# Pairing the first layer's gates and the later attention heads' projections as seven half-width products

## The chip, the cores and the metric

The kernel runs on one core of a Trainium2 chip. The metric is device time in microseconds. Before the change the median of three runs is 1910.99 us.

## The reference, cut to what matters

Two transformer blocks run one after the other on x of 512 tokens and 1024 features, all in fp32. The first block is:

```
h = rmsnorm(x, norm_mix_g);  proj = h @ w_in      # mLSTM q,k,v,o; attention q,k,v; gates g_a,g_b
y_a = mlstm(...)                                  # 4 heads
y_b = dilated window attention                    # 3 groups x 8 heads; head pairs hp = 0..3
merged = sigmoid(g_a) * (y_a @ w_proj_a) + sigmoid(g_b) * (y_b @ w_proj_b)
x = x + merged @ w_out
x = x + (silu(hf @ w_gate) * (hf @ w_up)) @ w_down    # hf = rmsnorm(x, norm_ffn_g)
```

The second block mixes gated linear attention and sparse attention and has its own feed-forward. The change doesn't touch it.

## The kernel before, in words

**Units.** Every weight matrix is cut into units of 1024 x 128 (eight pieces of 128 x 128, 512 KB). `unit_order` writes out the order by hand: 0 is the first. A unit with activations transposed (features on partitions, 512 tokens as columns) gives 128 output features. fp32 accuracy comes from a split into two fp32r parts: for each of the eight k a unit issues WH x XH, WH x XL and WL x XH (`products`, lines 1561 to 1563). That is 24 matmuls of 512 columns.

**Preparing a weight.** SP loads the unit into one of three RAW buffers (`load`, five units ahead). ACT copies it to WH (`split`, line 2064), and DVE (line 2467) or POOL (line 3267) writes WL = RAW - WH, two units ahead. WH and WL have three buffers each, which the code counts as six halves of 512 columns (`place_weights`). `lo_on_pool` gives POOL the odd units of some kinds.

**Pairs.** In the two feed-forwards most gate and up units already run in pairs. A pair is two neighbouring units seen as a 2 x 2 block matrix, tokens split in halves of 256. Seven products replace eight (Winograd's form of Strassen's scheme): `pair_products`, lines 1637 to 1639, 7 products of 12 matmuls of 256 columns. The seven weight operands ("chunks", half a unit each) are `a11, a12, s1, a22, s2, s4, s3`. Four of them are sums or differences made in place in the raw buffers (`chunk_add`, DVE). ACT copies each chunk to its WH half (line 2073), and DVE writes its WL half (line 2499). The activations' seven forms lie in AR. The products are put together by `pair_keep` (ACT), `pair_held` and `pair_add` (DVE) from four PSUM banks.

**The stages that matter here.** (1) mLSTM, four heads, with the projections of the next head as fill. (2) ga/pa: eight gate units `ga` and eight projection units `pa` in turn, `ga0 pa0 ga1 ...`, with four PSUM banks. (3) Attention: four head pairs hp of four query blocks. While hp is worked on, the nine q, k, v units of hp + 1 are the fill (`Fill`, a quarter of a unit at a time); for hp = 3 the eight `gb` units are. At the end of a block stand, in this order, the scores of the next block on PE, its softmax on DVE, its exponentials on ACT, and the PV product and the transposes of P. The fill has banks 0 and 1 only. Banks 2 and 3 hold scores, 4 the unfolded strips, 5 the PV product, and 6 and 7 transposes. (4) `pb`: eight units of 512 x 128, merged with `gb`, then the eight `out` units, which add to XT. XT stays in SBUF from the start until then.

Every engine runs its own list in order and waits on semaphores, so an instruction that waits holds everything behind it on its engine. The evictions of `qa, ka, va, gb, ga` read PSUM once and multiply by RB (the root, DVE lines 2613 and 2614).

Of the kernel before, what the change touches and what calls it, by code (L numbers as in the profile page):

```python
# [8 lines left out]
S = 512  # L9
# [13 lines left out]
LO_ON_POOL = ()  # L23
WARM_START = 9
# [34 lines left out]
def unit_order():  # L59
# [100 lines left out]

def lo_on_pool(i):

    return i % 2 == 1 and i > 3 and i != 7 and UNITS[i][0] in BUSY_DVE or i == AT["gate2", 1, 0]
# [11 lines left out]
def pair_start(i):  # L175

    name, j = UNITS[i][:2]
    if name[-1] == "2":
        return i - j % 2 if name in ("gate2", "up2") and "2" in PAIRED and j >= PAIR_FROM else None
# [3 lines left out]
def place_weights():  # L183
# [3 lines left out]
    for i in range(len(UNITS)):  # L187
# [10 lines left out]
        elif p == i:  # L198
            chunks = [((i, c), (h + c,), ("prod", i, c)) for c in range(7)]
        else:  # L200
            continue
# [10 lines left out]
def place_raw():  # L212
# [3 lines left out]
    for i, (name, j, k0, nk) in enumerate(UNITS):  # L216
        if name in ("if", "small2"):
            continue
        x = order.pop(0)
# [49 lines left out]
class Order:  # L269
# [35 lines left out]
    small_products = small_evict = small_select = keep_warm = gates_products = gates_evict = gates_select = none  # L305
    pair_products = pair_keep = pair_held = pair_add = pair_silu = pair_hi = pair_lo = none
# [109 lines left out]
def ahead(e, i):  # L416
    if i + 2 < len(UNITS):
        e.split(i + 2)
# [201 lines left out]
def mlstm(e):  # L620
# [25 lines left out]
    for h in range(4):  # L646
# [6 lines left out]
        fill.quarters(12 if h else 8)  # L653
        for t in range(4):
            e.hold((*SB, OB)[t], "numer", h, t)
        e.numerators(h)
        fill.quarters(6)
        e.normed(h)
        e.turns_apart = h < 3
        fill.quarters((6, 10, 10, 10)[h])  # L660
        if h == 3:
            mlstm_scores(e, 4)
# [31 lines left out]
def attention_blocks(e):  # L694
# [3 lines left out]
    at, e.turns_apart = unit_of("qa", 1), True  # L698
    for m, (hp, b) in enumerate(items):
        if b == 0:  # L700
            n = 9 if hp < 3 else 8
            fill = Fill(e, range(at, at + n), 4 if hp < 3 else 7)
            at += n
# [18 lines left out]
        if hp and b == 0:  # L722
            e.hold(4, "unfolded", hp - 1)
# [12 lines left out]
    e.hold(4, "unfolded", 3)  # L736
# [6 lines left out]
    fill.drain(True)  # L743
# [11 lines left out]
def attention(e):  # L755
# [4 lines left out]
    for j in range(8):  # L760
        unit(e, unit_of("ga", j))
        unit(e, unit_of("pa", j))
# [4 lines left out]
    attention_blocks(e)  # L767
# [24 lines left out]
def pair_steps(at, end):  # L792
# [3 lines left out]
    for i in range(at, end):  # L796
        nk, p = UNITS[i][3], pair_start(i)
        if p == i:
            steps += [("pair", i, c) for c in range(7)]
# [327 lines left out]
def build(nc, xT_d, wst_d, con_d, col_d, relb_d, oh_d, wa2_d, w1_d, w2_d, out_d, scr_d, mx_d):  # L1127
# [6 lines left out]
    with ExitStack() as ctx:  # L1134
        def sb(name, shape, dt=f32):
            return ctx.enter_context(nc.sbuf_tensor(name, shape, dt))

        XT = sb("XT", [128, 8, 512])
# [16 lines left out]
        RC = sb("RC", [128, 16])  # L1155

# [21 lines left out]
        pool_done = {n: signal("pool_" + n) for n in ("norm", "mlstm", "ffn", "gla")}  # L1178
        raw_in = [signal(f"raw_in{i}", 16) for i in range(NR)]
# [5 lines left out]
        wa2_in, w1_in, w2_in = signal("wa2_in", 16), signal("w1_in", 16), signal("w2_in", 16)  # L1185
        out_done = [signal(f"out_done{i}", 16) for i in range(2)]
# [33 lines left out]
        def plain(which, j, n=512):  # L1220

            at_ = H_at + 2048 * (8 * "HH HL AH AL".split().index(which) + j)
            return nc.alloc_sbuf_tensor_at(f"{which}plain{j}", [128, n], f32, offset=at_)[:, :]
# [44 lines left out]
        sgt = SS[0][:, 0:512]  # L1268
# [64 lines left out]
        def raw(i):  # L1333

            return RAW[:, R_SLOT[i], :]
# [8 lines left out]
        twice_held = bass.AP(HELD.tensor, HELD.offset, [list(HELD.ap[0]), [0, 2], [1, 256]])  # L1344

# [43 lines left out]
        def gate_tile(i):  # L1389
# [4 lines left out]
            return {"ga": sgt, "gb": gb3[:, j, :], "mg": SGT, "mn": SN3[:, j, :]}[name]  # L1394
# [45 lines left out]
        class Sync(Order):  # L1440
# [17 lines left out]
            def load(s, i):  # L1458
# [8 lines left out]
                d.then_inc(*raw_in[R_SLOT[i]].next("raw", i))  # L1467

# [63 lines left out]
        class Tensor(Order):  # L1532
# [87 lines left out]
            def pair_products(s, sfx, i, c):  # L1620
# [3 lines left out]
                          4: (("sum_z", i), 256), 5: (("sum", i), 256), 6: (("sum_w", i), 0)}[c]  # L1624
                out = PS[:, s.bank[key], o:o + 256]
                if c in (0, 1, 2, 6):
                    s.free(*key)
                elif c == 4:
                    pe.wait_ge(*at("kept", i))
                pe.wait_ge(*at("lo", i, c))  # L1630
                wh, wl = chunk(WH, i, c), chunk(WL, i, c)
                for m in range(4):
# [101 lines left out]
            def after(s, i, p):  # L1734
# [1807 lines left out]
```

## Time and profile before

| | |
|---|---|
| runs | 1910.97, 1910.99, 1911.03 us |
| span of the profiled execution | 1909.1 us |
| granted TensorE clock | 1.000 (2.4 GHz) |
| PE busy | 1898.5 us, 99% |
| DVE, ACT, POOL busy | 66%, 39%, 14% |

The span is that of one profiled execution. Its whole time isn't listed apart; the median of the runs is 1.9 us above the span, which is what lies around it. A busy share of a pipelined PE says only that matmuls follow one another; the distance between two starts gives their price.

### The profile page before, as it was taken

What the parts mean: (1) busy time and instruction counts of PE and PEld (TensorE: products, weight loads), DVE (VectorE), ACT (ScalarE), POOL (GpSimd) and SP (SyncE); (2) the same over time, 40 slices, a digit from 0 to 9 for tenths busy, and PEclk for the clock granted to TensorE, in tenths of its full rate; (3) what the DMA queues carried; (4) which work ended last, traced back from release to release, by engine and by line L of the source; (5) the groups of instructions that cost most, each with busy time, mean ns of one, the idle gap of its engine ahead of it and who ended that gap; (6) DMA issues with size and microseconds to landing.
All of it is one profiled execution on the core that took longest, in us unless ns stands there. A gap on an engine that the chain in (4) does not pass through costs nothing.

```text
span 1909.1 us, 26308 instructions
## 1 busy us (share of the span) xinstructions
PE 1898.5 (99%) x10599; PEld 1591.0 (83%) x10599; DVE 1255.4 (66%) x1894; ACT 735.3 (39%) x1265; POOL 265.1 (14%) x156
## 2 busy tenths in 40 slices
PE   9999999999999999999999999999999999999998
PEld 7788888888888888999997778877777878899998
DVE  7777543345455748777776756766776667887874
ACT  6332322233334444344435522224444354444442
POOL 0211210111111113000004001121111133100002
PEclk9999999999999999999999999999999999999999
DMA  5322233232321323233333222322121322333332
GB/s 177 102 70 85 88 86 115 89 99 67 89 67 45 115 91 104 78 106 102 114 108 103 77 67 78 100 79 65 56 67 40 116 79 87 100 100 100 100 130 81
DMA packets 53472, 172.77 MB, mean 90 GB/s; under 512 B 5963, under 2 KB 10643, under 8 KB 53352
## 3 DMA queue, kind: packets, MB, share of 16 engines
q1 hardware_dynamic: 52912, 170.66, 28.8%
q8 instruction: 84, 1.38, 0.3%
q10 hardware_dynamic: 440, 0.44, 0.1%
q14 instruction: 36, 0.29, 0.1%
HBM read 168.86 MB, written 2.22 MB: 90 GB/s over the span
## 4 chain that ended last, share of the span: by engine, by line
PE 94%; DVE 3%; ACT 1%; POOL 1%; issue 0%; DVEq 0%
PE PS L1561 22%; PE PS L1563 22%; PE PS L1562 22%; PE PS L1637 5%; PE PS L1639 5%; PE PS L1638 5%; PE PS L1983 1%; PE PS L2005 1%; PE PS L1780 1%; PE PS L1795 1%; PE PS L1961 1%; PE PS L1841 1%; PE PS L1827 1%; PE PS L1818 1%; PE PS L1748 1%; POOL XT L3338 1%
## 5 line engine op out<-in xcount | busy, mean ns | idle before, releaser
L1561 PE MATMUL PS<-HH,WH 128*128 128x512 f32 x1124 | 444.0, 395 | 0.8 <-DVE WL L2467 0.7
L1563 PE MATMUL PS<-HH,WL 128*128 128x512 f32 x1124 | 438.0, 390 | 0.0
L1562 PE MATMUL PS<-HL,WH 128*128 128x512 f32 x1124 | 437.4, 389 | 0.0
L2064 ACT ACTIVATE WH<-RAW 128x1024 fp32r<-128x1024 f32 (+2 forms) x256 | 261.1, 1020 | 336.4 <-PE PS L1563 271.4
L2467 DVE TENSOR_TENSOR WL<-RAW,WH 128x1024 fp32r<-128x1024 f32 (+2 forms) x195 | 251.2, 1289 | 113.7 <-ACT WH L2064 112.0
L1561 PE MATMUL PS<-AH,WH 128*128 128x512 f32 x816 | 323.7, 397 | 0.0
L1563 PE MATMUL PS<-AH,WL 128*128 128x512 f32 x816 | 318.1, 390 | 0.0
L1562 PE MATMUL PS<-AL,WH 128*128 128x512 f32 x816 | 317.6, 389 | 0.0
L1561 PEld LDWEIGHTS PS<-HH,WH 128*128 128x128 f32 x1124 | 211.1, 188 | 49.7 <-issue 4.2
L1563 PEld LDWEIGHTS PS<-HH,WL 128*128 128x128 f32 x1124 | 211.0, 188 | 45.1
L1562 PEld LDWEIGHTS PS<-HL,WH 128*128 128x128 f32 x1124 | 211.2, 188 | 42.2 <-issue 0.2
L3267 POOL TENSOR_TENSOR WL<-RAW,WH 128x1024 fp32r<-128x1024 f32 (+1 forms) x61 | 139.0, 2279 | 740.1 <-ACT WH L2064 740.1
L1637 PE MATMUL PS<-AR,WH 128*128 128x256 f32 x784 | 219.6, 280 | 0.0
L1639 PE MATMUL PS<-AR,WL 128*128 128x256 f32 x784 | 218.8, 279 | 0.0
L1638 PE MATMUL PS<-AR,WH 128*128 128x256 f32 x784 | 218.8, 279 | 0.0
L1561 PEld LDWEIGHTS PS<-AH,WH 128*128 128x128 f32 x816 | 153.2, 188 | 37.1 <-issue 6.5
L1563 PEld LDWEIGHTS PS<-AH,WL 128*128 128x128 f32 x816 | 153.2, 188 | 33.0
L1562 PEld LDWEIGHTS PS<-AL,WH 128*128 128x128 f32 x816 | 153.4, 188 | 30.5 <-issue 0.5
L2613 DVE TENSOR_TENSOR AR<-PS,RB 128x512 f32<-128x512 f32 (+2 forms) x117 | 84.3, 723 | 134.5 <-PE PS L1563 128.0
L2073 ACT ACTIVATE WH<-RAW 128x512 fp32r<-128x512 f32 x196 | 119.4, 624 | 93.3 <-DVE RAW L2486 36.7
L1637 PEld LDWEIGHTS PS<-AR,WH 128*128 128x128 f32 x784 | 147.2, 188 | 1.1
L1638 PEld LDWEIGHTS PS<-AR,WH 128*128 128x128 f32 x784 | 146.7, 187 | 1.1
(360 smaller groups left out, 2260.7 us busy)
## 6 DMA issues: line engine op xcount, KB each, us to landing
RAW<-wst SPq DMA_DIRECT2D x292, 512.0 KB, 3.6
RAW<-wst SPq DMA_DIRECT2D x16, 256.0 KB, 2.6
RAW<-wst SPq DMA_DIRECT2D x8, 384.0 KB, 3.1
XT<-xT SPq DMA_DIRECT2D x3, 512.0 KB, 7.3
out<-XT SPq DMA_DIRECT2D x4, 384.0 KB, 2.5
AR<-mx SPq DMA_DIRECT2D x4, 256.0 KB, 6.2
AR<-scr SPq DMA_DIRECT2D x16, 64.0 KB, 4.3
AR<-scr SPq DMA_DIRECT2D x8, 128.0 KB, 4.8
```

The costliest lines, as they stand in the source:

```text
L1561: T.matmul(out, wh, XH[:, k, :], start=k == 0, stop=False)
L1562: T.matmul(out, wh, XL[:, k, :], start=False, stop=False)
L1563: m = T.matmul(out, wl, XH[:, k, :], start=False, stop=k == nk - 1)
L1637: T.matmul(out, wh[:, w], xh, start=m == 0, stop=False)
L1638: T.matmul(out, wh[:, w], xl, start=False, stop=False)
L1639: t = T.matmul(out, wl[:, w], xh, start=False, stop=m == 3)
L1748: t = T.transpose(PS[:, b, q * 128:(q + 1) * 128], src[:, q * 128:(q + 1) * 128], ident())
L2064: t = A.activation(whole(WH, i, n), raw(i)[:, 0:n], ACT.Copy, scale=1.0)
L2073: t = A.activation(chunk(WH, i, c), raw_chunk(i, c), ACT.Copy, scale=1.0)
L2467: t = V.tensor_tensor(whole(WL, i, n), raw(i)[:, 0:n], f(whole(WH, i, n)), ALU.subtract)
L2613: return V.tensor_tensor(dst, src, rb, ALU.mult)
L3267: t = G.tensor_tensor(whole(WL, i, n), raw(i)[:, 0:n], f(whole(WH, i, n)), ALU.subtract)
```

## The change

Twenty pairs are added to those of the feed-forwards (`MIXED`): four in `ga`, four in `gb`, and four in the nine projection units of each of hp 1, 2 and 3 (the ninth stays whole). `ga` and `pa` now come two and two. The pairs' products run in the order a11, a12, s1, a22, s2, s3, s4 (`PAIR_ORDER`), so that three banks do: the product of s3 goes into the half of `sum_z` that `pair_keep` has read. In attention `sum_z` is bank 4, and the unfolded strips move to bank 5.

The half sums of the activations (T1, T4, T5, T6 of each of four m) are made in mLSTM's last head: `t_sums` (DVE, two scalings of 512 columns and four sums of 256), `t_hi` (ACT, 1024), `t_lo` (POOL, 1024). Their high part TXH lies on XT, so `reload_x` loads XT again (2 MB, four DMAs of 512 KB on SP's queue) once the product s3 of the last `gb` pair is done, ahead of the loads of pb5 and later.

In the new pairs POOL writes all seven WL halves and does two of the four chunk sums; DVE does the other two. A pair's outputs go to SBUF first (`pair_middle`, `pair_sum`), and `pair_out` multiplies them by RB from there. There are two more raw buffers from hp 1's projections to the `gb` units, on the free halves of AL. The list of fill is one `Stream` of steps for ga/pa and attention, of which `Share` hands out 32 steps for a head and 28 for the last.

```diff
-    for j in range(8):
+    for j in range(0, 8, 2):
         add("ga", j)
+        add("ga", j + 1)
         add("pa", j)
+        add("pa", j + 1)
...
+PAIR_ORDER = (0, 1, 2, 3, 4, 6, 5)
+ADD_ON_POOL = (5, 6)
+def mixed_pairs():
+    starts = [AT["ga", j, 0] for j in range(0, 8, 2)] + [AT["gb", j, 0] for j in range(0, 8, 2)]
+    starts += [AT["qa", hp, 0] + x for hp in (1, 2, 3) for x in (0, 2, 4, 6)]
+    return {p + n: p for p in starts for n in (0, 1)}
...
+class Stream:
+    def prepare(self):
+        e = self.e
+        while self.chunks and all(self.done.get(y, -1) < self.n for y in W_BEFORE[self.chunks[0]]):
+            while self.n_add < min(2, len(self.chunks)):
+                e.chunk_add(*self.chunks[self.n_add])
+                self.n_add += 1
+            self.n_add -= 1
+            y = self.chunks.pop(0)
+            e.chunk_hi(*y)
+            e.chunk_lo(*y)
+            if y[0] >= self.end:
+                break
+    def step(self):
+        e, (kind, i, x) = self.e, self.steps[self.n]
+        if kind == "pair":
+            if x == 0:
+                e.load(i + 5)
+                e.load(i + 6)
+            if x == 0 and len(e.ring) == 2:
+                e.hold(4, "sum_z", i)
+            elif x in (0, 1, 2):
+                e.sum_bank("sum" if x else "sum_z", i + (x == 2))
+            e.pair_products("1", i, x)
...
+        now, self.queue = self.queue, []
+        for i2, y in now:
+            e.pair_out(i2, y)
...
+        self.prepare()
...
+            if x == 0:
+                e.pair_keep(i)
+            elif x == 6:
+                e.pair_middle(i)
+            if x in (6, 5):
+                e.pair_sum(i, int(x == 6))
+                self.queue.append((i, int(x == 6)))
...
+            def pair_middle(s, i):
+                V.tensor_tensor(held[:, 0:256], z[:, 256:512], kept[:, 0:256], ALU.add).then_inc(
+                    *dve_done["attn"].next("held", i))
+                dve.wait_ge(*at("held", i))
+                t = V.tensor_tensor(held[:, 256:512], z[:, 0:256], held[:, 0:256], ALU.add)
+                t.then_inc(*bank_read.next("free", "sum_z", i))
...
+            def chunk_lo(s, i, c):            # POOL
+                pool.wait_ge(*at("hi", i, c))
+                t = G.tensor_tensor(chunk(WL, i, c), raw_chunk(i, c), f(chunk(WH, i, c)), ALU.subtract)
+            def chunk_add(s, i, c):           # POOL
+                pool.wait_ge(*at("added", i, 4))
+                if c == 5:
+                    pool.wait_ge(*at("lo", i, 1))
+                    t = G.tensor_tensor(r1[:, 512:1024], r1[:, 512:1024], r1[:, 0:512], ALU.add)
+                else:
+                    pool.wait_ge(*at("lo", i, 3))
+                    t = G.tensor_tensor(r2[:, 512:1024], r1[:, 0:512], r2[:, 512:1024], ALU.add)
...
+            def reload_x(s):
+                sp.wait_ge(*at("prod", unit_of("gb", 6), 6))
+                for g in range(4):
+                    d = S.dma_start(XT[:, 2 * g:2 * g + 2, :], xT_d[:, 2 * g:2 * g + 2, :])
...
-        e.hold(4, "unfolded", 3)
+        e.hold(OB, "unfolded", 3)
```

The DVE's own `chunk_add` for s2 is as before: it waits for the WL half of a11, which POOL now writes.

## Rows read from the trace of the kernel before

**Rows 1.** The page: engines' busy time, then the chain that ended last.
```profile
PE 1898.5 (99%) x10599; PEld 1591.0 (83%) x10599; DVE 1255.4 (66%) x1894; ACT 735.3 (39%) x1265; POOL 265.1 (14%) x156
...
PE 94%; DVE 3%; ACT 1%; POOL 1%; issue 0%; DVEq 0%
```

**Rows 2.** Windows (columns: PE, PEld, DVE, ACT, POOL busy, clock, DMA): stages around the change.
```profile
200.00:300.00 100.00, 100.00 (x458) 82.34 (x457) 48.08 (x68) 24.99 (x35) 15.54 (x8) 1.00 0.34 99
...
286.00:370.00 84.00, 84.00 (x372) 69.57 (x372) 30.99 (x38) 20.08 (x23) 2.40 (x1) 1.00 0.35 104
...
429.00:494.00 65.00, 64.95 (x402) 53.39 (x400) 31.29 (x45) 20.95 (x51) 11.92 (x5) 1.00 0.29 77
...
625.00:652.00 27.00, 26.93 (x119) 21.97 (x118) 22.94 (x31) 11.20 (x17) 4.32 (x3) 1.00 0.40 127
```

**Rows 3.** Timeline of PE: first matmul of unit pa0, and of the next unit.
```profile
288.67 0.39 PE L1561 MATMUL PS<-AH,WH 128*128 128x512 f32 x1
...
294.11 0.39 PE L1561 MATMUL PS<-HH,WH 128*128 128x512 f32 x1
```

**Rows 4.** Timeline of PE: first and 84th matmul of a feed-forward pair, and the next.
```profile
853.38 0.28 PE L1637 MATMUL PS<-AR,WH 128*128 128x256 f32 x1
...
863.15 0.28 PE L1639 MATMUL PS<-AR,WL 128*128 128x256 f32 x1
863.27 0.40 PE L1561 MATMUL PS<-HH,WH 128*128 128x512 f32 x1
```

**Rows 5.** Chain in order of time: scores, transposes and PV at block ends.
```profile
414.01 1.08 PE PS L1818 x12
415.08 1.02 PE PS L1841 x16
416.11 1.02 PE PS L1827 x8
429.38 0.87 PE PS L1818 x12
...
494.09 0.87 PE PS L1818 x12
```

**Rows 6.** POOL by line and shape, whole span.
```profile
L3267 POOL TENSOR_TENSOR WL<-RAW,WH 128x1024 fp32r<-128x1024 f32 x53 | 127.8, 2412 | 685.7 <-ACT WH L2064 685.7
...
L3267 POOL TENSOR_TENSOR WL<-RAW,WH 128x512 fp32r<-128x512 f32 x8 | 11.2, 1402 | 54.4 <-ACT WH L2064 54.4
```

**Rows 7.** Timeline of POOL in the pb stage, then six additions after another.
```profile
634.80 1.29 POOL L3267 TENSOR_TENSOR WL<-RAW,WH 128x512 fp32r<-128x512 f32 x1 [3.71 <-ACT WH L2064]
...
1553.18 9.82 POOL L3338 TENSOR_TENSOR XT<-XT,AR 128x512 f32<-128x512 f32 x6 [3.50 <-DVE AR L3172]
```

**Rows 8.** Timeline of DVE beside the POOL work of rows 7.
```profile
634.99 1.65 DVE L2651 TENSOR_TENSOR AR<-AR 128x512 f32<-128x512 f32 x1
...
1558.36 0.74 DVE L3172 SCALAR_TENSOR_TENSOR AR<-AR,COL,PS 128x512 f32<-128x512 f32 x1
1559.02 1.13 DVE L2446 SCALAR_TENSOR_TENSOR HL<-XT,COL,HH 128x512 fp32r<-128x512 f32 x1
```

**Rows 9.** DVE by line and shape, 750 to 1000 us (feed-forward pairs).
```profile
L2486 DVE TENSOR_TENSOR RAW<-RAW 128x512 f32<-128x512 f32 x14 | 9.6, 685 | 0.0
...
L2555 DVE TENSOR_TENSOR AR<-PS,AR 128x256 f32<-128x256 f32 x14 | 5.8, 417 | 0.0
```

**Rows 10.** The page's groups: ACT's copy of a chunk.
```profile
L2073 ACT ACTIVATE WH<-RAW 128x512 fp32r<-128x512 f32 x196 | 119.4, 624 | 93.3 <-DVE RAW L2486 36.7
```

**Rows 11.** Timeline of ACT after the scores of rows 5.
```profile
417.70 0.51 ACT L2249 ACTIVATE AR<-AR 128x256 f32<-128x256 f32 x1 [7.06 <-DVE AR L2904]
...
420.44 1.05 ACT L2064 ACTIVATE WH<-RAW 128x1024 fp32r<-128x1024 f32 x1
```

**Rows 12.** DMA queue (packets, MB, share of 16 engines), and issue to landing.
```profile
q1 hardware_dynamic: 52912, 170.66, 28.8%
...
RAW<-wst SPq DMA_DIRECT2D x292, 512.0 KB, 3.6
```

More of the change, by code:

```diff
@@ L177, in pair_start @@
     name, j = UNITS[i][:2]
+    if i in MIXED:
+        return MIXED[i]
     if name[-1] == "2":
@@ L198, in place_weights @@
         elif p == i:
-            chunks = [((i, c), (h + c,), ("prod", i, c)) for c in range(7)]
+            order = PAIR_ORDER if i in MIXED else range(7)
+            chunks = [((i, c), (h + n,), ("prod", i, c)) for n, c in enumerate(order)]
         else:
@@ L218, in place_raw @@
             continue
+        if i == AT["qa", 1, 0]:
+            order += [NR, NR + 1]
+            user[NR] = user[NR + 1] = [("unit", AT["pa", 7, 0])]
+        elif i == AT["pb", 0, 0]:
+            order = [x for x in order if x < NR]
         x = order.pop(0)
@@ L305 @@
     small_products = small_evict = small_select = keep_warm = gates_products = gates_evict = gates_select = none
+    t_sums = t_hi = t_lo = pair_middle = pair_sum = pair_out = reload_x = none
     pair_products = pair_keep = pair_held = pair_add = pair_silu = pair_hi = pair_lo = none
@@ L759, in attention @@
     e.load_bias(1)
-    for j in range(8):
-        unit(e, unit_of("ga", j))
-        unit(e, unit_of("pa", j))
+    stream = Stream(e, unit_of("ga", 0), unit_of("gb", 7) + 1, 4)
+    for _ in range(60):
+        stream.step()
     e.ring = [0, 1]
@@ L789, in ffn, with __init__, finish @@
         unit(e, i)
-def pair_steps(at, end):
+class Stream:
+    def __init__(self, e, at, end, ready):
+        self.e, self.end, self.n = e, end, 0
+        self.steps, self.done = pair_steps(at, end, True), {}
+        for n, (kind, i, x) in enumerate(self.steps):
+            self.done[("prod", i, x) if kind == "pair" else ("unit", i)] = n
+        self.chunks = [(i, c) for i in range(at, end + 2) for c in ([None] if pair_start(i) is None else
+                                                                    PAIR_ORDER if pair_start(i) == i else [])][ready:]
+        self.n_add, self.queue = 0, []
+    def prepare(self):
[21 more added lines that the diff above has]
+            e.pair_products("1", i, x)
+        else:
+            if x[0] == 0:
+                e.load(i + 5)
+                e.sum_bank("sum", i)
+            e.products(i, x)
+        now, self.queue = self.queue, []
+        for i2, y in now:
+            e.pair_out(i2, y)
+            if UNITS[i2 + y][0] in PARTS:
+                e.later.append(("unit", i2 + y, 1))
+        self.prepare()
+        if kind == "unit":
+            if x[-1] % 4 == 3:
+                flush(e, not e.turns_apart)
+            if x[-1] == 7:
+                evict(e, i)
+        else:
+            if x in (1, 3, 4, 5):
+                flush(e, not e.turns_apart)
+            if x == 0:
[5 more added lines that the diff above has]
+                self.queue.append((i, int(x == 6)))
+            if x == 5 and len(e.ring) == 2:
+                e.taken += 1
+        self.n += 1
+    def finish(self):
+        e = self.e
+        for i2, y in self.queue:
+            e.pair_out(i2, y)
+            if UNITS[i2 + y][0] in PARTS:
+                e.later.append(("unit", i2 + y, 1))
+        self.queue = []
+        self.prepare()
+        while self.chunks:
+            self.n += 1
+            self.prepare()
@@ L795, in pair_steps @@
+def pair_steps(at, end, quarters=False):
     steps = []
@@ L798, in pair_steps @@
         if p == i:
-            steps += [("pair", i, c) for c in range(7)]
+            steps += [("pair", i, c) for c in (PAIR_ORDER if quarters else range(7))]
+        elif p is None and quarters:
+            steps += [("unit", i, range(2 * q, 2 * q + 2)) for q in range(4)]
         elif p is None and nk == 6:
@@ L1344, in build, with temps, evicted @@
         twice_held = bass.AP(HELD.tensor, HELD.offset, [list(HELD.ap[0]), [0, 2], [1, 256]])
+        T_IN, T_SUM = [plain("AH", 6, use="scaled"), plain("AH", 7, use="scaled")], plain("AL", 6, 1024, "sums")
+        GA_TEMPS = parts(4608, 512, 512, 512, 512)
+        AT_TEMPS = [plain("AH", j, use="held") for j in (4, 5, 6, 7)]
+        SPARE = [plain("AL", j, 1024, use="raw") for j in (4, 6)]
+        def temps(i):
+            if i not in MIXED:
+                return KEPT, HELD, GATE if UNITS[i][0][0] == "g" else [UP, UP]
+            t = GA_TEMPS if UNITS[i][0] == "ga" else AT_TEMPS
+            return t[0], t[1], t[2:4]
+        def evicted(i):
+            return ("out", i) if i in MIXED else ("free", "sum", i)
         def f_tiles(i):
@@ L1847, in unfold @@
                 pe.wait_ge(*at("strips", hp))
-                t = T.matmul(PS[:, 4, 0:64], con("unfold"), strips, start=True, stop=True)
+                t = T.matmul(PS[:, OB, 0:64], con("unfold"), strips, start=True, stop=True)
                 t.then_inc(*pe_done["attn"].next("unfolded", hp))
```

218 lines of the change are left out of this document (186 added, 32 removed).

## The prediction

> **What bounds the kernel now.** I read the page first. PE is busy 99% of 1909.1 us and holds 94% of the chain that ended last; no other engine has over 3% of it [rows 1]. A busy share alone isn't enough, so I took windows over the stages that the change touches: PE has no idle time in ga/pa or in attention, and 0.07 us of 27 in pb [rows 2]. The clock is 1.00 throughout. So a matmul taken away shortens the kernel by its pitch, as long as nothing makes PE wait. POOL is almost idle there (2.4 us of 84 in ga/pa, 11.9 of 65 in a head), and DVE is under half busy [rows 2]. The question is whether the two can carry what the change gives them.
>
> **What the change takes from PE.** A whole unit is 24 matmuls; the next unit starts 294.11 - 288.67 = 5.44 us later [rows 3], so two units cost 10.88 us. A pair of seven products is 84 matmuls of half width, and the work behind it starts 863.27 - 853.38 = 9.89 us later [rows 4]: 0.118 us a matmul, 1.41 us a product. The pair saves 0.99 us. Twenty pairs save 19.8 us: 4.0 in ga, 11.9 in the three heads, 4.0 in gb. That is the most that can come back.
>
> **What it adds, pair by pair.**
> - *POOL.* Seven WL halves and two chunk sums, nine operations of 512 columns. Alone one takes 1.29 us [rows 7]; the mean of the eight such operations is 1.40 [rows 6]. The low value is free of DVE's share, which I add apart: 9 x 1.29 = 11.6 us.
> - *DVE with two SBUF inputs.* Two chunk sums and two `pair_out`, four operations of 0.69 [rows 9]. They don't run beside POOL. In rows 8 an addition of normally 0.69 took 1.65 us: it started 0.19 after POOL's operation of 1.29 and ended 0.55 after it. Where POOL ran six operations on end with one such DVE operation to each, it took 9.82 us, 1.64 each [rows 7], and DVE's took 1.13 [rows 8]: one DVE operation costs POOL 1.64 - 1.29 = 0.35 us. I take 0.4, as strided outputs of groups 1 and 2 are longer: 4 x 0.4 = 1.6 us a pair. The bounds are 0 (DVE falls into POOL's gaps) and its whole 0.69.
> - *DVE from PSUM.* Three operations of 256 columns at 0.42 and two of 512 at 0.69 [rows 9], 2.6 us, beside POOL. They replace two evictions.
> - *ACT.* Seven copies of 0.62 [rows 10] for two of 1.05 [rows 11], and one `pair_keep`: some 2.7 us more per pair. ACT is a third busy (20.9 of 65) [rows 2], so only its order matters, below.
>
> The Trainium skill (SBUF - State Buffer, who interferes with whom) says that a DVE instruction with two SBUF inputs and a GpSimd instruction that reads SBUF exclude each other for the whole instruction. The trace agrees that they exclude each other; that DVE costs POOL its whole 0.69 is not what the six operations show.
>
> **ga/pa.** A period is now one pair and two whole `pa`, 9.89 + 10.88 = 20.8 us. POOL and the port need 11.6 + 1.6 us, and DVE's WL of two `pa` and two one-source scalings some 2 us more. Followed chunk by chunk from the end of the first `pa` (s1 and a22 get their halves there, s2 and s3 when the second ends and the pair starts, at 0): the WL of s2 is done at 0.62 + 1.29 and some waiting, 2.1 us, and PE asks at 5.7; POOL's sum for s4 and the WL of s3 end at 4.9, and PE asks at 7.1; the WL of s4 ends at 6.3, and PE asks at 8.5. DVE's operations take about 1 us of these 2.2 to 3.6 us. Four banks leave time. Stall 0, gain 4.0.
>
> **Attention, a head.** PE now needs 28 x 1.41 = 39.6 us for four pairs, 5.4 for the whole unit, and what attention itself costs: 64.7 (494.09 - 429.38, scores to scores [rows 5]) less nine units (49.0), 15.7 us. That is 60.7 us.
>
> (a) *Throughput.* The 28 products with three of four block ends are 39.6 + 11.8 = 51.4 us. POOL and DVE on the port need 4 x (11.6 + 1.6) = 52.8. They fall 1.4 us behind, and catch up during the whole unit.
>
> (b) *Order.* At a block's end ACT waits for DVE's softmax and then makes the exponentials: scores end at 415.09 [rows 5], ACT is back at weights at 420.44 [rows 11], 5.35 us later, while PE is back at products after the transposes and PV, 2.04 us later [rows 5]. Six halves let five products be ready ahead. ACT is back 3.3 us into them, the next chunk's copy and WL take 0.62 + 1.29, so it is ready at 5.2, or 5.8 with a DVE operation in between; PE asks at 5 x 1.41 = 7.07. No stall by that alone. But `sum_z` has one bank. The next pair's first product waits for `pair_middle`, whose two operations (0.84) can start only after the product of s3; and DVE's list has the next pair's sum for s2 ahead of them, which waits for POOL's WL of a11 of that pair. After that WL come on average 0.65 for POOL's next operation, 0.69 and 0.84: 2.2 us, where the margin is 1.3 to 1.9. I take 0.9 us of stall per head. Bounds: 0, and with no lead at all 1.29 + 0.69 + 0.84 = 2.8 us at every pair, of which a POOL that gains from each stall lets about half stand, 1.5.
>
> So a head stalls 1.4 + 0.9 = 2.3 us. The gb stage has the same four pairs under the last head; I give it 2.3 as well. Four stages: 9.2 us.
>
> **The rest.** `t_sums` is 4 x (2 x 0.42 + 4 x 0.42) = 10 us of DVE, with 4 x 1.05 on ACT and 4 x 2.4 on POOL [rows 6]. Its cover is the last mLSTM head, where DVE is 48% and POOL 16% busy [rows 2]: 0, at most 1 us. Without the cover it would be 10 us. `reload_x` puts 2 MB ahead of pb5's load on SP. At 170.66 MB in 28.8% of 1909.1 us, 310 GB/s [rows 12], 2 MB take 6.8 us. Issued 1.4 before gb ends, they are in by 7.4 after it at the latest (2 us of latency), and pb5's 256 KB by 8.5. ACT asks for it at the start of pb3, 3 x 2.72 = 8.2 us in, and PE at 13.6: 0, at most 3. The wait of `out` for XT comes over 20 us in. The unfolded strips in bank 5 wait for a PV product read before on the same list: 0. The two more raw buffers keep SP's loads early; a load of 512 KB takes 3.6 us [rows 12] and has a pair's time.
>
> **Sum.** 19.8 - 9.2 = 10.6 us. Span 1909.1 - 10.6 = 1898.5; with the 1.9 us around it, the same as the gap to the median of the runs shown, 1900.4 us.
>
> **Rivals.**
> - *All is hidden* (0.22). DVE finds gaps in POOL, and the lead of five products absorbs the bursts. For it: over a whole head the port needs 52.8 + 2 of 60.7 us. Against it: the deficit within the 28 products. 1911.0 - 19.8 = 1891.2 us.
> - *The one bank decides: slower* (0.15). Each of the 16 pairs in attention waits 1.5 us for the chain WL of a11, sum for s2, `pair_middle`. 19.8 - 4 x 1.4 - 24 = -9.8: 1920.8 us. It decides from (19.8 - 5.6) / 16 = 0.9 us a pair. For it: POOL has nearly no slack, so the lead is often short. Against it: after a stall the lead is longer.
> - *The port is held for DVE's whole operation* (0.08). 16 x 4 x (0.69 - 0.4) = 18.6 us more: 1919.0 us. Against it: rows 7 and 8. This is what the Trainium skill's rule (SBUF - State Buffer, who interferes with whom) would make of it.
> - *The reload makes pb wait* (0.10): 3 us more, 1903.4 us. For it: the margin at ACT is under 1 us.
> - The forecast has 0.45, with a range of its own of 1896 to 1906.
>
> **How the numbers follow.** Measurements of this kernel tell 0.2%, 3.8 us, from no change: 1907.2 to 1914.8 us. Faster: the forecast but for 0.03, all hidden and the late reload, 0.74. Same: that 0.03, and 0.05 of the two slower cases, should they come in part. Slower: the other 0.18 of them. The range starts a little under all hidden, 1890.5, and goes up to 1912, half way into the slower ones, which leaves out about 0.18.
>
> **What would show it.** PE: 20 x 84 more matmuls of 256 columns, 20 x 48 fewer of 512, at unchanged pitch. ga/pa shorter by 4.0 us. Scores to scores near 63.0 in place of 64.7; under 61 says all is hidden, over 65 one of the slower cases. POOL near 12.9 to 13.5 us a pair, with single operations of 1.6 to 2.0 us where DVE cuts in, and DVE operations with two SBUF inputs of up to 1.9. PE's first wait at a pair's first product, released by DVE, says (b); PE waits inside a pair, released by POOL's WL, say (a). I am wrong if POOL's operation on a RAW and a WH half runs much slower when it never pauses, or if ACT's list, not POOL's, is late.

## The result, and the profile after

The kernel got slower: 1957.86 us (median of four, 1956.66 to 1958.07) against 1911.01 us for the kernel before beside it, ratio 1.0243, 95% interval 1.0231 to 1.0256. The forecast was 1900.4 us, and 1957.86 lies outside the range too. The page of the kernel after, busy times and the chain that ended last:

```profile
PE 1901.3 (97%) x11319; PEld 1626.4 (83%) x11319; DVE 1350.3 (69%) x2034; ACT 781.6 (40%) x1389; POOL 488.9 (25%) x324
...
PE 82%; DVE 7%; POOL 4%; ACT 3%; issue 3%; DMA 0%; SPq 0%; DVEq 0%; ACTq 0%; POOLq 0%
```

Against [rows 1], PE was to be 19.8 us less busy and is 2.8 us more, and its share of the chain fell from 94% to 82%. The span is 1956.0 us. PE's idle time is 1956.0 - 1901.3 = 54.7 us, before 10.6: 44.1 us of new waits. Its busy time should have been 1898.5 - 19.8 = 1878.7 us and is 22.6 us more. So -19.8 + 44.1 + 22.6 = 46.9 us, which is the whole difference of the spans. Windows of the kernel after (PE, PEld, DVE, ACT, POOL busy, clock, DMA): ga/pa, two stretches inside the heads, then 280 to 760 us as a whole:

```profile
286.00:370.00 84.00, 79.55 (x491) 71.91 (x489) 41.01 (x56) 26.53 (x42) 40.54 (x32) 0.98 0.35 108
380.00:445.00 65.00, 55.23 (x425) 50.64 (x425) 40.17 (x51) 25.16 (x61) 51.09 (x36) 0.95 0.26 82
445.00:517.00 72.00, 63.86 (x544) 59.31 (x544) 48.37 (x70) 29.61 (x75) 52.33 (x36) 0.98 0.24 74
280.00:760.00 480.00, 435.58 (x3081) 392.19 (x3081) 293.48 (x405) 189.93 (x408) 267.59 (x192) 0.97 0.26 84
```

In [rows 2] PE had no idle time and a clock of 1.00. Now it has both losses, and no engine is full: in a head DVE is busy 62 to 67%, POOL 73 to 79%. What PE waited for between 280 and 760 us (total, times, longest):

```profile
PE PS L1818 <- DVE AHheld L2755: 18.1, 10, 3.1
PE PS L1740 <- DVE AHheld L2767: 8.0, 3, 3.5
PE PS L1818 <- POOL WL L3564: 5.2, 5, 3.3
PE PS L2033 <- DVE AR L3215: 4.3, 1, 4.3
PE PS L1939 <- DVE VT L2854: 3.2, 3, 1.1
PE PS L2019 <- DVE AR L3244: 1.8, 1, 1.8
```

L2755 is `pair_middle`, L2767 `pair_sum`, L3564 POOL's `chunk_lo`, L2854 `pair_out`, and L3215 reads the unfolded strips out of bank 5. The first row, 18.1 us, is pairs' first products that wait for the one bank of `sum_z`. The second, 8.0 us, is whole units (L1740) that wait for a sum bank which `pair_sum` has yet to read. The whole list has 28 waits and comes to 44.4 us. The timeline of one wait of the first row, at the end of a block of hp 1, where hp 2's projections are the fill:

```profile
485.47 0.68 DVE L3192 TENSOR_REDUCE AR<-AR 128x2 f32<-128x512 f32 x1
...
486.18 0.51 ACT L2457 ACTIVATE AR<-AR 128x256 f32<-128x256 f32 x1 [3.80 <-DVE AR L3192]
...
489.43 1.14 ACT L2265 ACTIVATE WH<-RAW 128x512 fp32r<-128x512 f32 x2
...
490.13 5.88 POOL L3564 TENSOR_TENSOR WL<-RAW,WH 128x512 fp32r<-128x512 f32 x4 [5.94 <-ACT WH L2265]
...
491.96 1.67 DVE L2690 TENSOR_TENSOR RAW<-RAW 128x512 f32<-128x512 f32 x1 [1.26 <-POOL WL L3564]
493.56 0.41 DVE L2752 TENSOR_TENSOR AHheld<-PS,AHheld 128x256 f32<-128x256 f32 x1
...
494.00 0.42 DVE L2755 TENSOR_TENSOR AHheld<-PS,AHheld 128x256 f32<-128x256 f32 x1
...
494.48 0.39 PE L1818 MATMUL PS<-HH,WH 128*128 128x256 f32 x1 [2.35 <-DVE AHheld L2755]
```

Read it from below. PE waits for `pair_middle` (0.41 and 0.42 us). That stands behind DVE's sum for s2 (L2690), which waited 1.26 us for POOL's WL of a11 and then took 1.67 us where it takes 0.69 alone [rows 9]. POOL had stood idle for 5.94 us, because ACT had stood 3.80 us at its exponentials waiting for DVE's softmax and came back to weights at 489.43. Each engine idles, each because of the next one, and all lists are in order.

ACT's late return is not new. After the same block's scores in the kernel before (461.13 to 462.28 us) ACT is back at weights 8.2 us later, as it is here (481.21 to 489.43), because the merge of the last head stands ahead of this block's softmax on DVE:

```profile
467.23 0.51 ACT L2249 ACTIVATE AR<-AR 128x256 f32<-128x256 f32 x1 [8.03 <-DVE AR L2904]
...
470.48 1.05 ACT L2064 ACTIVATE WH<-RAW 128x1024 fp32r<-128x1024 f32 x1
```

PE didn't wait there in the kernel before, which had no bank that hangs on this chain.

After the wait PE runs at half speed for a while. Its timeline there, and two windows:

```profile
494.94 0.32 PE L1818 MATMUL PS<-HH,WH 128*128 128x256 f32 x1
495.06 0.41 PE L1819 MATMUL PS<-HL,WH 128*128 128x256 f32 x1
495.26 0.42 PE L1820 MATMUL PS<-HH,WL 128*128 128x256 f32 x1
...
498.46 0.28 PE L1820 MATMUL PS<-HH,WL 128*128 128x256 f32 x1
```
```profile
480.00:490.00 10.00, 10.00 (x110) 9.43 (x109) 6.65 (x9) 4.45 (x14) 4.19 (x4) 1.00 0.31 107
490.00:500.00 10.00, 7.64 (x51) 7.44 (x50) 7.51 (x10) 3.25 (x7) 9.73 (x7) 0.83 0.00 1
```

From 495.06 to 498.25 a matmul comes every 0.213 us, before and after every 0.12: 1.2 GHz for 3.3 us, then 2.4 again. That stretch costs 3.3 x (1 - 0.12 / 0.213) = 1.4 us on top of the wait of 2.35.

The lower clock is not the whole of the 22.6 us. In windows of 10 us from 280 to 660 us the shares of granted clock that are missing add up to 30.6 us at 1.2 GHz, in eight stretches. By the same ratio that is 13 to 14 us. Another part is the pitch of the new pairs, which is not that of the feed-forward pairs. The ga pairs of a run below (e14), in which PE doesn't wait there, show it:

```profile
304.36 0.28 PE L1822 MATMUL PS<-HH,WH 128*128 128x256 f32 x1
...
314.44 0.40 PE L1744 MATMUL PS<-AH,WH 128*128 128x512 f32 x1
```

That pair takes 10.08 us where [rows 4] has 9.89, 0.120 us a matmul, so it saves 0.80 us and not 0.99. Twenty pairs make 3.8 us. No run shows why the pitch differs. The rest, some 5 us, I put down to the 28 waits themselves: the last matmul before a wait is counted busy for 0.28 or 0.39 us, where the next would have started after 0.12 or 0.23, 0.16 us each. This last part is an estimate.

Scores to scores went from 64.7 us [rows 5] to 72.3 and 74.5 in hp 1 and 2, and from 58.9 to 70.1 in hp 0. The first scores came 4.0 us late instead of 4.0 early, and from 591 us on another 14.3 us were lost.

### The profile page after: what moved, and what is told of

It is laid out like the page before. It is cut to its first block, busy times and chain, and to the rows that moved or that the text cites. A ratio compares the mean times of both kernels' runs of the same rounds, so it can differ in the third digit from the quotient of the medians.

```text
span 1956.0 us, 28353 instructions
## 1 busy us (share of the span) xinstructions
PE 1901.3 (97%) x11319; PEld 1626.4 (83%) x11319; DVE 1350.3 (69%) x2034; ACT 781.6 (40%) x1389; POOL 488.9 (25%) x324
## 3 DMA queue, kind: packets, MB, share of 16 engines
q8 instruction: 90, 1.47, 0.3%
## 4 chain that ended last, share of the span: by engine, by line
PE 82%; DVE 7%; POOL 4%; ACT 3%; issue 3%; DMA 0%; SPq 0%; DVEq 0%; ACTq 0%; POOLq 0%
PE PS L1740 18%; PE PS L1742 17%; PE PS L1741 17%; PE PS L1828 5%; PE PS L1830 5%; PE PS L1829 5%; POOL WL L3564 3%; PE PS L1818 1%; ACT AR L2457 1%; PE PS L1819 1%; PE PS L1820 1%; PE PS L2175 1%; PE PS L2197 1%; PE PS L1971 1%; PE PS L1986 1%
## 5 line engine op out<-in xcount | busy, mean ns | idle before, releaser
L1740 PE MATMUL PS<-HH,WH 128*128 128x512 f32 x804 | 318.2, 396 | 10.2 <-DVE AHheld L2767 7.0
L1740 PE MATMUL PS<-AH,WH 128*128 128x512 f32 x816 | 324.0, 397 | 1.1 <-DVE AHheld L2767 1.0
L2256 ACT ACTIVATE WH<-RAW 128x1024 fp32r<-128x1024 f32 (+2 forms) x215 | 217.6, 1013 | 248.2 <-PE PS L1742 182.6
L1742 PE MATMUL PS<-HH,WL 128*128 128x512 f32 x804 | 313.9, 390 | 0.0
L1741 PE MATMUL PS<-HL,WH 128*128 128x512 f32 x804 | 313.3, 390 | 0.0
L2265 ACT ACTIVATE WH<-RAW 128x512 fp32r<-128x512 f32 x290 | 174.7, 624 | 178.6 <-DVE RAW L2694 36.9
L3555 POOL TENSOR_TENSOR WL<-RAW,WH 128x1024 fp32r<-128x1024 f32 (+1 forms) x45 | 101.1, 2247 | 423.1 <-ACT WH L2256 423.1
L1740 PEld LDWEIGHTS PS<-HH,WH 128*128 128x128 f32 x804 | 151.3, 188 | 47.2 <-DVE AHheld L2767 8.8
L1740 PEld LDWEIGHTS PS<-AH,WH 128*128 128x128 f32 x816 | 153.2, 188 | 38.8 <-issue 6.5
L1742 PEld LDWEIGHTS PS<-HH,WL 128*128 128x128 f32 x804 | 151.2, 188 | 32.6
L1741 PEld LDWEIGHTS PS<-HL,WH 128*128 128x128 f32 x804 | 151.4, 188 | 30.3 <-issue 0.2
L3564 POOL TENSOR_TENSOR WL<-RAW,WH 128x512 fp32r<-128x512 f32 x94 | 131.0, 1414 | 87.8 <-ACT WH L2265 87.7
```

The costliest lines, as they stand in the source:

```text
L1740: T.matmul(out, wh, XH[:, k, :], start=k == 0, stop=False)
L1741: T.matmul(out, wh, XL[:, k, :], start=False, stop=False)
L1742: m = T.matmul(out, wl, XH[:, k, :], start=False, stop=k == nk - 1)
L2256: t = A.activation(whole(WH, i, n), raw(i)[:, 0:n], ACT.Copy, scale=1.0)
L2265: t = A.activation(chunk(WH, i, c), raw_chunk(i, c), ACT.Copy, scale=1.0)
L3555: t = G.tensor_tensor(whole(WL, i, n), raw(i)[:, 0:n], f(whole(WH, i, n)), ALU.subtract)
```

## The experiments

All are the kernel after with the edit shown, except where the diff names another. Times are medians; the kernel before ran beside each, at 1911.0 to 1911.1 us. A span is given where a profile is compared.

**ga's pairs alone**

```diff
-    starts = [AT["ga", j, 0] for j in range(0, 8, 2)] + [AT["gb", j, 0] for j in range(0, 8, 2)]
-    starts += [AT["qa", hp, 0] + x for hp in (1, 2, 3) for x in (0, 2, 4, 6)]
+    starts = [AT["ga", j, 0] for j in range(0, 8, 2)]
...
-            fill = Share(stream, 32, 4) if hp < 3 else Share(stream, 28, 7)
+            fill = Share(stream, 36, 4) if hp < 3 else Share(stream, 32, 7)
```

> Only the four ga pairs are left; the projections of heads and the gb units are whole units as before (with the new order of ga and pa, the half sums, the five raw buffers and the reload of x). All theories: the heads go back to 64.7 us. If the ga stage alone lost what its trace says (scores 4.0 us later than before), 1915 us; if the new pairs' cost in attention also rests on something else that stays here (reload, raw buffers, strips' bank), more than 1920 us.

1919.61 us, ratio 1.0045 (1.0030 to 1.0060), between the two expectations. (`reload_x` waits here for the last gb unit.) Heads are back at 59.0, 64.7 and 64.7 us, so the sixteen other pairs carry 1957.9 - 1919.6 = 38.3 us of the loss. The first scores come 6.8 us later than before the change, although all four ga pairs are there; in the kernel after it was 4.0. Its waits:

```profile
PE PS L1817 <- POOL WL L3563: 4.6, 4, 3.4
PE PS L2009 <- DVE AR L2926: 2.1, 1, 2.1
```

The second row has its reason on DVE and POOL, just ahead of the first scores (timelines):

```profile
372.54 1.23 DVE L2674 TENSOR_TENSOR WL<-RAW,WH 128x1024 fp32r<-128x1024 f32 x1 [1.72 <-ACT WH L2255]
373.68 2.60 DVE L3037 TENSOR_SCALAR AR<-AR 128x512 f32<-128x512 f32 x1
```
```profile
373.53 2.47 POOL L3554 TENSOR_TENSOR WL<-RAW,WH 128x1024 fp32r<-128x1024 f32 x1 [11.35 <-ACT WH L2255]
```

A scaling with one SBUF tensor as input, 0.43 us in the kernel before, took 2.60 us: POOL's operation began 0.15 us ahead of it and ended at 376.00, DVE's at 376.28. In the kernel before that POOL operation fell a little after the scaling. In the kernel after the unit behind pa7 is a pair, this operation isn't there, and PE doesn't wait at the first scores. By the Trainium skill (SBUF — State Buffer, Who interferes with whom) such a scaling may take both of DVE's port pairs, one of which is POOL's, and whoever comes second is blocked; this row agrees.

**Bias loads late**

The first wait in ga/pa has another cause. DVE's first row and SP's queue in the kernel after:

```profile
307.88 0.69 DVE L2686 TENSOR_TENSOR RAW<-RAW 128x512 f32<-128x512 f32 x1 [8.35 <-DMA RAW<-wst]
```
```profile
291.27 0.80 SPq L1639 DMA_DIRECT2D RAW<-wst  x2
292.17 7.09 SPq L1673 DMA_DIRECT2D AR<-scr  x12
```
```profile
310.72 0.55 PE L1818 MATMUL PS<-TXH,WH 128*128 128x256 f32 x1 [3.28 <-POOL WL L3564]
```

Twelve small loads of attention's bias held SP for 7.09 us ahead of the next raw units. A pair frees its raw units in one go and needs both for s1, so they were late by that much.

```diff
-    e.load_bias(0)
-    e.load_bias(1)
     stream = Stream(e, unit_of("ga", 0), unit_of("gb", 7) + 1, 4)
-    for _ in range(60):
+    for n in range(60):
         stream.step()
+        if n == 46:
+            e.load_bias(0)
+            e.load_bias(1)
```

> The changed kernel, but the twelve loads of the first two heads' bias are issued from the fourth ga pair on, not ahead of the ga/pa stage. Theory D (with three raw buffers the second ga pair's raw unit is queued behind them and lands 8 us late, which costs PE's first wait of 3.3 us and the clock after it): ga/pa 5 to 7 us shorter, about 1951 us. Rival (the raw unit is late by the three buffers alone): unchanged, 1957 us.

1952.07 us, 1.0215 (1.0200 to 1.0231): 5.8 us back, as Theory D said. In the profiles PE's idle time fell by 4.2 us, 2.8 of them in the waits for POOL's WL (5.2 to 2.4), and its busy time by 1.7, about what the stretch at the lower clock behind the first wait cost: 310 to 320 us has a granted clock of 0.83 in the kernel after.

**WL of a11, s1 and s2 on DVE; all on DVE**

```diff
+LO_ON_DVE = (0, 2, 4)
...
-                if i in MIXED:
+                if i in MIXED and c not in LO_ON_DVE:
                     return
...
-                if i not in MIXED:
+                if i not in MIXED or c in LO_ON_DVE:
                     return
```

> The changed kernel, but DVE writes the WL halves of a11, s1 and s2 of the new pairs, and POOL the other four. Theory A (DVE's list: the sum for s2 waits for POOL's WL of a11 and stands ahead of pair_middle, so the one sum_z bank comes free late): that sum no longer waits for POOL, and most of PE's 18.1 us of waits for pair_middle go; with the clock that they cost, about 1925 us. Theory B (POOL's rate and the port shared with DVE are what is short): POOL does six operations a pair for nine and the same port time is needed by fewer operations: also faster, but by less, about 1940 us, and PE's waits for pair_middle stay above 10 us. Rival (DVE itself is full, 67 to 73% busy there): 1957 us or more.

1995.95 us, 1.0445 (1.0428 to 1.0463): 38 us worse, in spite of the relief for POOL. Theories A and B, both of which said faster, are out in this form; only the rival's side is left. POOL's busy time in 372 to 580 us falls from 155.8 to 90.4 us, and DVE becomes the list on which all stands:

```profile
PE PS L1819 <- DVE AHheld L2756: 35.1, 11, 4.3
PE PS L1741 <- DVE AHheld L2768: 14.4, 4, 5.2
```

With all seven WL and all four sums on DVE (`LO_ON_DVE = range(7)`, `ADD_ON_POOL = ()`):

> All seven WL halves and all four sums of the new pairs on DVE, as in the feed-forward pairs; POOL gets none. No operation waits for the port. If the port were the cost, this would be the fastest, under 1950 us. Theory A': every WL in DVE's list waits for ACT's copy behind the exponentials, and the list is also longest: slower than the split, 2000 to 2030 us.

1969.16 us (one run), which meets neither expectation: it isn't the fastest, and not slower than the split. DVE has more to do than with three WL, 169.9 us of the 208 between 372 and 580 against 156.1, and the kernel is 27 us faster. What went away is POOL beside it, and with it the hand-overs between the two lists; no run separates the two. DVE's sum for s2 by shape in 280 to 660 us, first in the kernel after, then with the split, then all on DVE (busy, mean ns):

```profile
L2690 DVE TENSOR_TENSOR RAW<-RAW 128x512 f32<-128x512 f32 x10 | 14.7, 1469 | 23.8 <-POOL WL L3564 23.8
```
```profile
L2691 DVE TENSOR_TENSOR RAW<-RAW 128x512 f32<-128x512 f32 x9 | 14.9, 1656 | 0.0
```
```profile
L2691 DVE TENSOR_TENSOR RAW<-RAW 128x512 f32<-128x512 f32 x10 | 6.8, 683 | 0.0
```

This DVE operation of 0.68 us takes 1.47 to 1.66 in the mean when it falls among POOL's. The prediction priced what DVE costs POOL (0.35 us) and left out what POOL costs DVE, 0.8 to 1.0 us.

**The sum for s2 on POOL**

```diff
-ADD_ON_POOL = (5, 6)
+ADD_ON_POOL = (4, 5, 6)
...
+                if c == 4:
+                    pool.wait_ge(*at("lo", i, 0))
+                    t = G.tensor_tensor(r1[:, 0:512], r1[:, 0:512], r2[:, 0:512], ALU.subtract)
```

> The changed kernel, but POOL makes the sum for s2 as well, ten operations a pair for nine, and DVE's list never waits for POOL. Theory A': PE's 18.1 us of waits for pair_middle fall under 5 us, and POOL's waits grow by less; 1930 to 1942 us. Theory B (POOL's rate): 16 pairs x 1.3 us more on the engine that is short, 1957 us or more.

1946.14 us, 1.0182 (1.0165 to 1.0199): 11.7 us back, though POOL has 1.3 us more a pair. That is 4 us short of what Theory A' said, and 11 from Theory B.

```profile
PE PS L1740 <- DVE AHheld L2767: 10.8, 3, 4.8
PE PS L1818 <- POOL WL L3564: 9.4, 12, 2.2
...
PE PS L1818 <- DVE AHheld L2755: 3.0, 3, 1.6
```

The wait for `pair_middle` goes from 18.1 us to 3.0. `pair_sum` is later (8.0 to 10.8), and so is POOL itself: 9.4 us in twelve small pieces.

**Reading the banks first** (`out_of_banks` holds the lines taken out below)

```diff
+        if kind == "pair" and x in (6, 5):
+            self.out_of_banks(i, x)
         self.prepare()
...
-            elif x == 6:
-                e.pair_middle(i)
-            if x in (6, 5):
-                e.pair_sum(i, int(x == 6))
-                self.queue.append((i, int(x == 6)))
```

> The changed kernel, but pair_middle and pair_sum stand ahead of the chunk sums of the same step in every list. Nothing else moves. Theory A: PE's waits for pair_middle fall from 18.1 us to under 5, and part comes back as waits for WL; about 1935 us. Theory B: the waits only change their name, 1952 to 1960 us.

1942.18 us, 1.0162 (1.0147 to 1.0178): 15.7 us back with the same work on the same engines, 7 us short of Theory A's time.

```profile
PE PS L1822 <- POOL WL L3568: 7.7, 6, 3.5
PE PS L1943 <- DVE VT L2858: 6.4, 3, 2.2
...
PE PS L1822 <- DVE AHheld L2759: 1.6, 1, 1.6
```

`pair_middle` (L2759) goes from 18.1 us to 1.6. In exchange DVE's list now stands waiting for the product of s3, and what is behind it, such as `pair_out` to the tokens that attention transposes, is later by some 3 us in all. That is the part of the gain that comes back as other waits. Both edits of e1 and e2 together:

> The two edits together: WL of a11, s1 and s2 on DVE as in the run that split WL, and pair_middle and pair_sum ahead of the chunk sums as in the run that moved them. The split alone made the kernel 38 us slower, the order alone 16 us faster. Theory A' (what costs is that DVE's list holds, ahead of the reads of PSUM, work that waits for another engine: POOL's WL in the changed kernel, ACT's copies behind the exponentials in the split): with the reads ahead the split loses most of its harm, 1935 to 1950 us. Rival (DVE is simply full with the split): still above 1970 us.

1976.26 us, 1.0341 (1.0326 to 1.0357): 19.7 us better than the split alone, 34 worse than the order alone. The rival's side came true: with the split most of the harm stays when the reads of PSUM stand first, so order alone doesn't explain it. The order helps with either division of the work; three WL more on DVE, with POOL at work beside it, hurt in either order.

**Matmuls in the waits**

```diff
+            def keep_clock(s, n):
+                pe.wait_ge(*at("free", *s.holder[OB]))
+                for _ in range(n):
+                    T.matmul(PS[:, OB, 256:512], ident(), con("ba", 0, 256), start=True, stop=True)
```

> The changed kernel with three matmuls of 256 columns in plain fp32 (about 0.5 us each) on constants, into a free half of bank 5, ahead of the first product of each pair and whole unit in attention but the first of each head. They do no useful work; 12 places, 18.6 us of PE. Theory C (a wait of 2 us and more is followed by a stretch at the lower clock, which costs some 20 us in all): the waits they fill were idle anyway, so at most 8 us are added, and the clock gives back 5 to 15 us: 1945 to 1955 us, clock above 0.995. Rival (the clock falls whatever PE does in the waits): 1962 us or more.

It came to 45 added matmuls in 15 places (90 records, 22.0 us). 1954.79 us, 1.0229 (1.0214 to 1.0244). Span 1952.1 us, idle 37.9, busy 1914.2, of which 1892.2 are the kernel's own work: 9.1 us less than in the kernel after, for the same instructions. Idle time fell by 16.8. So -16.8 - 9.1 + 22.0 = -3.9 us, the difference of the spans. The windows between 280 and 660 us now show four stretches at the lower clock, 13.6 us in all, in place of eight with 30.6. By the ratio above that is 7 to 8 of the 9.1 us. So the lost clock does hang on PE's waits, and work put into them gives some of it back, but at a price that eats nearly all. The time is just inside Theory C's range.

**All the good edits, then fewer pairs**

e12 is banks first, the sum for s2 on POOL and late bias loads, with all twenty pairs. e13 is e12 with twelve pairs: four in ga, two in each head and in gb, `Share` 34 and 30.

> All twenty pairs; pair_middle and pair_sum ahead of the chunk sums, the sum for s2 on POOL, the bias loads later. If the three costs are apart, the gains of 15.7, 11.7 and 5.8 us overlap only in the waits for pair_middle: 1927 to 1935 us. If another bound is close behind (POOL with ten operations a pair and DVE waiting for the port), little is left of the second: 1935 us and above. In neither case faster than before the change.

1932.90 us, 1.0115 (1.0101 to 1.0129). The three edits gave 33.2 us singly and give 25.0 together, as the first theory said. 21.8 us of the loss stay.

> As the run with the three edits, but only two pairs in each head's projections (units 1 and 2, 5 and 6 of the nine) and two in gb, twelve pairs in all. 8 pairs fewer save 7.9 us less on PE. If the cost in attention grows faster than the number of pairs (POOL and DVE can keep up with half of them), this is faster than all twenty, 1910 to 1922 us; if every pair costs the same, the loss against the kernel before is halved in attention, 1921 to 1926 us.

1926.26 us, 1.0082 (1.0067 to 1.0097). Half the pairs in attention, and only 6.6 us less loss, at the edge of what "every pair costs the same" gave. Counted with the 0.80 us that a pair saves, the waits and the clock cost 21.8 + 16.0 = 37.8 us with twenty pairs and 15.2 + 9.6 = 24.8 with twelve: 1.9 and 2.1 us a pair. So the cost does go about with the number of pairs. Its longest waits:

```profile
PE PS L2024 <- DVE AR L3079: 4.6, 2, 2.6
PE PS L1745 <- POOL WL L3560: 4.5, 2, 3.4
PE PS L1745 <- DVE AHheld L2772: 4.4, 5, 1.6
```

The products of the pairs hardly wait any more. The whole units (L1745) and attention's own steps (L2024) do, behind the pairs' work on POOL and DVE.

**ga's pairs alone, made good**

e10 is ga's pairs with late bias loads and the split of WL, since DVE has room there. e14 adds two edits to it:

```diff
 def lo_on_pool(i):
+    if i in (AT["qa", 1, 0], AT["ka", 1, 0]):
+        return False
...
     fill(0.5)
+    fill.quarters(1)
     e.hold(OB, "unfolded", 3)
     e.unfold(3)
```

> Only the four ga pairs, as in the run before that had them alone (1919.6 us), with the bias loads issued later and with DVE writing WL of a11, s1 and s2. In ga/pa DVE has time, and ACT has no exponentials. Theory: the late raw unit's 5.8 us and the smaller waits for POOL's WL go, and 4.0 us of pairs are left against 1.7 us in pb and some 2 us at the first scores: 1910 to 1914 us. Theory A' with the split harmful everywhere: over 1916 us.

1911.36 us, 1.0002 (0.9993 to 1.0011). PE no longer waits inside ga/pa. It waits 1.6 us at the first scores, behind the same scaling (2.61 us here), and 1.3 us with the PV product behind the last head's unfolding, which needs the same bank 5.

> Built on e10 (pairs in ga alone, bias loads late, WL of a11, s1, s2 on DVE), where PE still waits four times after 280 us: 1.55 us at attention's first scores, 1.31 us at the first unfolding of the last head, and 0.15 and 0.24 us elsewhere. Two edits: (1) the WL of the two units behind pa7 are both DVE's, none POOL's, so that the scaling of 0.42 us that took 2.61 us beside POOL's 2.48 us is free again; (2) one more quarter unit of fill stands ahead of the last head's unfolding. My theory (a DVE operation that stands beside a POOL operation is held until that ends): the scaling is back at 0.42, the first wait goes or falls under 0.3 us although DVE has 1.2 us of WL more ahead of it, and with the second wait gone the kernel takes 1911.4 - 2.5 = 1908.9 us, ratio 0.999, a little under the kernel before. Rival (DVE was simply full there, the scaling was held by something else): the added 1.2 us on DVE lengthen the first wait to some 2.7 us, and the time stays at 1911 to 1912 us.

1908.54 us (11 runs, 1908.30 to 1908.98) against 1911.06 (15 runs, 1910.86 to 1911.32), 0.9987 (0.9978 to 0.9996): the expectation to 0.4 us, and the only kernel here that beats the one before. The timeline of DVE and all that PE waits for after 280 us:

```profile
364.15 1.23 DVE L2679 TENSOR_TENSOR WL<-RAW,WH 128x1024 fp32r<-128x1024 f32 x1 [1.72 <-ACT WH L2260]
365.29 0.42 DVE L3042 TENSOR_SCALAR AR<-AR 128x512 f32<-128x512 f32 x1
365.82 0.69 DVE L2931 TENSOR_TENSOR AR<-AR,PS 128x512 f32<-128x512 f32 x1
366.42 1.22 DVE L2679 TENSOR_TENSOR WL<-RAW,WH 128x1024 fp32r<-128x1024 f32 x1
```
```profile
PE PS L2037 <- DVE AR L3219: 0.3, 1, 0.3
PE PS L2023 <- DVE AR L3253: 0.2, 1, 0.2
```

The scaling is at 0.42 us again. DVE was given 1.22 us more in front of the scores, and the wait went away, which the rival (DVE simply full) didn't allow. The gain of 2.8 us over e10 is about the two waits, 1.6 and 1.3.

## Why the prediction was wrong, step by step

- **Take from PE: right but for the pitch.** The matmuls went as counted (720 more instructions on PE). A new pair takes 10.08 us, not 9.89, so twenty save 16.0 us, not 19.8. In e14, where nothing waits, the first scores come at 367.40 in place of 370.36 us: 3.0 of the four pairs' 4.0 us. The four pitches are 0.8 of the rest, and 0.2 is there at 270 us already, ahead of ga.
- **ga/pa, "stall 0, gain 4.0": wrong by 8.0 us.** The text followed POOL and DVE chunk by chunk and not SP's queue, where 7.09 us of bias loads stood ahead of two raw units with only three buffers. PE waits 4.4 us there for POOL's WL (3.3, 0.7, 0.2 and 0.2), and one stretch at the lower clock adds some 1.5. Late bias loads give back 5.8 us. The loads of `load` were taken as early without a row for it.
- **(a) throughput, 1.4 us a head: not what decided.** PE's waits for POOL's WL inside a pair are 5.2 us in all, 4.4 of them in ga/pa and 0.8 in attention's first pair, where 5.6 stood in the sum for attention.
- **(b) the one bank, 0.9 us a head: the step that failed.** The mechanism was the right one, down to the chain WL of a11, sum for s2, `pair_middle`, and its size was wrong by a factor of five: ten waits for L2755, 18.1 us, where 0.9 x 4 = 3.6 stood in the sum. Taking the sum for s2 off DVE's list brought them to 3.0 us, reading the banks first to 1.6. The row above of 494 us says which terms were too small. PE came back to products at 484.70, and `pair_middle` was done at 494.42, 9.7 us later, where the prediction's own terms give 3.3 + 0.62 + 1.29 + 0.69 + 0.84 = 6.7 and PE asks at 7.1. Of the 3 us, 1.4 are ACT's: it came back 4.7 us into the products and not 3.3, since the prediction measured a block without the merge ([rows 5] and [rows 11]) for all four. 1.0 is the sum for s2, put at 0.69 us, which takes 1.67 among POOL's operations. The remaining 0.6 is mostly WL of a11. The average of 2.2 us after a WL was set against a margin, and the end of a block and the one bank were never added into one chain.
- **`pair_sum` and the whole units: no term.** Three waits of PE for L2767, 8.0 us. It is the same list of DVE, but another bank.
- **DVE costs POOL 0.35 to 0.4 us: about right for POOL, half of the price.** POOL's WL on RAW took 1.41 us in the mean, where 1.29 is the value alone. The other half is what POOL costs DVE, 0.8 to 1.0 us on the sum for s2. DVE's list holds the banks, so this is the half that PE sees. Rows 8 of the trace before had it: the 1.65 us were read, and only POOL's side was put into the sum.
- **The clock: no term at all.** It is some 14 us of the 46.9. Rows 2 show 1.00 all along, in stages where PE never waited.
- **"The unfolded strips in bank 5 ...: 0": wrong by 4.3 us.** The text looked at the strips waiting for the PV product. It is the PV product of the last block (L2033) that waits for DVE's read of the strips (L3215), and that read stood behind a sum for s2 of 1.67 us which itself had waited 2.5 us for POOL. In the kernel before the two had a bank each, and PE had no such wait. It is one wait of 4.3 us; a quarter unit of fill ahead of it leaves 0.3 (e14).
- **Attention's other steps: no term.** The transposes of tokens (for `pair_out`) and of P wait 3.2 + 1.0 + 1.8 us for DVE.
- **`t_sums` hidden, `reload_x` 0: right.** PE has no wait for TXH or TXL or for XT; the four reloads took 1.85 us of SP's queue, and loads of XT landed after 7.2 us in the median.
- **The rivals.** "The one bank decides" named place and chain. Its 1.5 us a pair came to 18.1 / 16 = 1.1, over the 0.9 from which it decides, and to 1.6 with `pair_sum`'s waits. It gave 1920.8 us and had 0.15; what it lacked is the 22.6 us of busy time and most of the waits in ga/pa and at attention's own steps. "The port is held for DVE's whole operation" is not what decided: POOL pays less than that, DVE pays more. "All is hidden" and the late reload are out.

What stays open: e12, with the three edits that helped, still loses 21.8 us, which its waits name but no run takes apart. And attention's pairs with two banks for `sum_z` were not tried, as the banks are all in use.

## What to carry to other kernels

When an idle engine is given work, price the collision from both sides, and give the larger price to the engine whose list holds what the busy engine waits for. On in-order lists look at what an instruction that waits stands in front of: moving the reads of PSUM ahead of the sums that wait was worth 15.7 us with no work changed. And a gain of 0.8 us per pair on an engine that is 99% busy is worth nothing if each pair then costs some 2 us in waits; here the lower clock behind the waits added 14 us to 44. Take such a gain only where the helpers have room, as in ga/pa, and check the queue of loads too. When you time a chain from a trace, take the latest of the blocks, not one of them. When two tiles come to share a bank, price both of the waits, each for the other.

## What the runs showed of the hardware

- TensorE's clock stood at 2.4 GHz (granted clock 1.00) in all the stages of the kernel before that rows show. In the kernel after it fell to 1.2 GHz eight times between 280 and 660 us, during a wait of PE or within some 1 us of one; these waits were of 1.8 to 4.3 us. At 494 us it fell 0.6 us after PE resumed from a wait of 2.35 us, for 3.3 us. The length of the wait doesn't decide alone: two waits of 2.03 us at 475 and 547 us and one of 3.50 at 586 had no drop (windows of 1.00), one of 1.95 us at 389 had (0.87).

```profile
585.63 0.50 PE L1740 MATMUL PS<-HH,WH 128*128 128x512 f32 x1 [3.50 <-DVE AHheld L2767]
```

- The same matmul of 256 columns comes every 0.118 us in the feed-forward pairs and every 0.120 in the new pairs, both at 2.4 GHz, and every 0.213 at 1.2.
- A DVE operation with two SBUF inputs that meets one of POOL's ends only after it: the sum for s2 goes from 0.69 us to 1.47 (mean) or 1.67 beside operations of 512 columns, and a scaling from 0.42 to 2.60 beside one of 1024. For two SBUF inputs, and for a scaling with one, this is what the Trainium skill says (SBUF — State Buffer, Who interferes with whom); that DVE loses more by it than POOL is this trace's.
- Twelve small loads (64 and 128 KB) held SP's queue 7.09 us, 0.59 each, while a unit of 512 KB takes some 0.4 to issue.
